# Sums of squares on quarters of the array, and a new order of the first loads, in a one-core decoder layer

## The reference

```python
mod = silu(c) @ w_ada + b_ada                      # shift1, scale1, gate1, shift2, scale2, gate2
h = x * (1 + scale1) + shift1
q, k, v, u_a, v_a = split(h @ w_in)                # each 1024 wide
attn = moba_attention(q, k_all, v_all, rel_bias)   # 8 heads; sample rows also see 256 cached rows
gm = gelu(u_a) * chunk_spatial_gate(layer_norm(gelu(v_a)))
mixed = concat(rms_norm(gm) * norm_a_g, rms_norm(attn) * norm_b_g)
x = layer_norm(ALPHA * x + gate1 * (mixed @ w_out))
h = x * (1 + scale2) + shift2
up = h @ w_up;  ff = silu(conv_a(up)) * conv_b(up) # causal convolution, width 3, d_ff 5504
y = layer_norm(ALPHA * x + gate2 * (ff @ w_down))
```

## Time and profile before

| | us |
|---|---|
| median of 3 executions | 1412.66 (1411.91 to 1414.5) |
| the profiled execution | 1412.51 |
| its span, first to last instruction | 1410.1 |
| TensorE busy | 1373.4 (97%) |
| VectorE busy | 841.1 (60%) |
| ScalarE busy | 569.1 (40%) |
| GpSimd busy | 103.7 (7%) |

### The profile page before, as it was taken

One profiled execution on the slowest core, in us unless ns is written; L12 is line 12 of the kernel. 1 busy time (PEld: TensorE's weight loads), 2 busy tenths in 40 slices (PEclk: granted clock), 3 DMA queues, 4 the chain that ended last, 5 costly groups with the idle time before them and its releaser, 6 DMA issues.

```text
span 1410.1 us, 29096 instructions
## 1 busy us (share of the span) xinstructions
PE 1373.4 (97%) x11354; PEld 1300.6 (92%) x11354; DVE 841.1 (60%) x1400; ACT 569.1 (40%) x842; POOL 103.7 (7%) x250
## 2 busy tenths in 40 slices
PE   5999999999999999999999999999999999999996
PEld 4989898899788888899999999999999999999995
DVE  2475556567866458565666454675665544766655
ACT  3532222253543236643444333444444333444443
POOL 1000000003221000110001000010010000101000
PEclk9999999999999999999999999999999999999997
DMA  9989988885789989775544545545545454454541
GB/s 374 380 334 383 344 337 310 331 284 170 258 280 336 340 308 345 266 284 212 187 156 158 173 162 164 163 149 178 164 146 182 158 168 162 147 181 166 173 136 67
DMA packets 89762, 324.92 MB, mean 230 GB/s; under 512 B 10637, under 2 KB 10637, under 8 KB 89296
## 3 DMA queue, kind: packets, MB, share of 16 engines
q1 hardware_dynamic: 82368, 297.05, 59.3%
q0 software_dynamic: 6880, 24.10, 4.9%
q10 hardware_dynamic: 432, 2.62, 0.5%
HBM read 318.05 MB, written 5.67 MB: 230 GB/s over the span
## 4 chain that ended last, share of the span: by engine, by line
PE 93%; DVE 2%; DMA 2%; ACT 1%; issue 1%; SPq 1%; DVEq 0%; ACTq 0%
PE ps L446 28%; PE ps L447 28%; PE ps L448 27%; PE ps L462 5%; DMA ada<-w_ada 1%; DMA raw<-w_in 1%; PE ps L753 1%; PE ps L624 0%; SPq L895 0%; ACT wH L973 0%; DVE wL L1356 0%; PE ps L554 0%; PE ps L651 0%; PE ps L672 0%; PE ps L475 0%
## 5 line engine op out<-in xcount | busy, mean ns | idle before, releaser
L1356 DVE TENSOR_TENSOR wL<-raw,wH 128x1024 fp32r<-128x1024 f32 x372 | 449.0, 1217 | 358.3 <-ACT wH L973 356.4
L973 ACT ACTIVATE wH<-raw 128x1024 fp32r<-128x1024 f32 x372 | 389.5, 1053 | 587.4 <-PE ps L448 568.3
L446 PE MATMUL ps<-hL,wH 128*128 128x288 f32 x2016 | 602.6, 299 | 5.0 <-DVE hL L1394 4.4
L447 PE MATMUL ps<-hH,wL 128*128 128x288 f32 x2016 | 600.4, 298 | 0.0
L448 PE MATMUL ps<-hH,wH 128*128 128x288 f32 x2016 | 598.6, 297 | 0.0
L446 PEld LDWEIGHTS ps<-hL,wH 128*128 128x128 f32 x2016 | 381.6, 189 | 19.2 <-issue 9.8
L447 PEld LDWEIGHTS ps<-hH,wL 128*128 128x128 f32 x2016 | 379.4, 188 | 0.5 <-issue 0.5
L448 PEld LDWEIGHTS ps<-hH,wH 128*128 128x128 f32 x2016 | 379.1, 188 | 0.0
L446 PE MATMUL ps<-ffL,wH 128*128 128x288 f32 x688 | 204.5, 297 | 0.0
L447 PE MATMUL ps<-ffH,wL 128*128 128x288 f32 x688 | 203.0, 295 | 0.0
L448 PE MATMUL ps<-ffH,wH 128*128 128x288 f32 x688 | 202.3, 294 | 0.0
(11 more groups left out here) (237 smaller groups left out, 1005.3 us busy)
## 6 DMA issues: line engine op xcount, KB each, us to landing
raw<-w_up SPq DMA_DIRECT2D x168, 512.0 KB, 3.5
ada<-w_ada SPq DMA_DIRECT2D x112, 512.0 KB, 6.2
raw<-w_down SPq DMA_DIRECT2D x83, 512.0 KB, 3.5
raw<-w_in SPq DMA_DIRECT2D x80, 512.0 KB, 7.5
adaX<-w_ada SPq DMA_DIRECT2D x40, 512.0 KB, 5.4
adaY<-w_ada SPq DMA_DIRECT2D x40, 512.0 KB, 7.3
raw<-w_out SPq DMA_DIRECT2D x32, 512.0 KB, 5.3
KV<-keys POOLq DMA_DIRECT2D x16, 512.0 KB, 5.6
```

Source lines behind the costliest of these rows:

```text
L446: nc.tensor.matmul(out, wH[:, w:w + P], rhs_lo(kk), start=start, stop=False)
L447: nc.tensor.matmul(out, wL[:, w:w + P], rhs_hi(kk), start=False, stop=False)
L973: nc.scalar.activation(wH[:, o:o + cols], raw[:, o:o + cols], ACT.Copy).then_inc(hi_done, 1)
L1356: vec_tt(wL[:, o:o + cols], raw[:, o:o + cols], wH[:, o:o + cols].bitcast(F32), ALU.subtract).then_inc(split_done, 1)
```

## The change

At the start:

- SyncE issues `w_in` slab 0 between the fourth and the fifth conditioning slab. The first rows of x come in two loads: tiles 0 and 1 on SyncE's queue after the eighth conditioning slab, tiles 2 and 3 on ScalarE's queue after the high part of slab 1.
- ScalarE and VectorE split slab 0 before the modulation. `modulate` does the samples first and then each k-tile's prompt part as one tensor_scalar (multiply and add), and for k-tile 0 and 1 the high part, the low part and TensorE's wait are made tile by tile (`h32_first`, `hH_first`, `h_first`). ScalarE's high part of slab 1 comes after these.
- The first two bursts come after slab 3 and slab 6, not 2 and 5; the turn of unit 1 moves from slab 6 to 7.

At the end of the input projection:

- "sum a" becomes eight matmuls with 32 columns of ones, four at a time on the four column quarters of the array (`quarter_sums`), a copy of the 128 rows of partial sums by ScalarE, and one full matmul over them (`joined_sums`); each sum is then 32 times too large, which the root's scale undoes. "sum ad" likewise. The samples' squares move from step 79 to 78; the quarters of "sum ad" come after slab 78, its joined sum after slab 79.
- The joined sum of "sum a" comes after slab 78. VectorE inverts the root and does `norm_prompt(0, 0)` at step 78. `norm_prompt(0, 1)` moves behind the split of slab S_OUT + 3, and `m_ready` now counts it, so mix tiles 4 to 7 wait for it and tiles 0 to 3 don't.
- `turn_v` uses banks 2, 3, 4 and then 5, 4, 3; the second three come after `past_scores(0)`. `scores(0)` waits for two groups, not four. `new_scores` comes after `out_slab(0)`, and its VectorE part (`new_logits`) after the mix tiles 4 to 7.
- GpSimd's second product comes right behind its first, ahead of the store of k and of the load of the second cached sequence.

```diff
-BURSTS = [2, 5, 8, 11, 14, 16] + [...]
+BURSTS = [3, 6, 8, 11, 14, 16] + [...]
...
@@ tensor
+            def quarter_sums(job, bank, ready, lo, hi):
+                pe.wait_ge(sq_ready, ready)
+                b = take(pe, job, bank)
+                for j in range(2):
+                    for c in range(4):
+                        mm = nc.tensor.matmul(b[32 * c:32 * c + 32, lo:hi], ones[:, 0:32], tile(proj, 32 + 4 * j + c, lo, hi), start=(j == 0), stop=(j == 1))
+                fill(mm, job)
+            def joined_sums(job, parts_job, bank, parts, lo, hi):
+                released(pe, parts_job)
+                b = take(pe, job, bank)
+                fill(nc.tensor.matmul(b[:, lo:hi], ones[:, :], parts, start=True, stop=True), job)
...
-                if g == 0:
+                if i == 0:
+                    arriving = lambda kk: pe.wait_ge(h_ready if kk else h_first, 1)
+                elif g == 0:
...
                 if i == 77:
-                    sum_squares("sum a", 5, 1, [tile(proj, k, 0, SEQ) for k in range(32, 40)], 0, SEQ)
-            turn_v(0, 0, 0)
-            turn_v(1, 0, 6)
-            turn_v(2, 0, 7)
-            sum_squares("sum ad", 5, 2, [tile(proj, k, SEQ, ROWS) for k in range(32, 40)], SEQ, ROWS)
+                    quarter_sums("quarters a", 5, 1, 0, SEQ)
+                if i == 78:
+                    joined_sums("sum a", "quarters a", 6, RRa[:, :], 0, SEQ)
+                    quarter_sums("quarters ad", 5, 2, SEQ, ROWS)
+            joined_sums("sum ad", "quarters ad", 7, RRd[:, :], SEQ, ROWS)
+            turn_v(0, 0, 2)
+            turn_v(1, 0, 3)
+            turn_v(2, 0, 4)
...
@@ sync
             for a in range(HALF):
+                if a == HALF // 2:
+                    load(0, io["w_in"], 0, 0)
                 load_ada(a, a)
-            for s in range(RING):
+            sp.dma_start(xT[:, 0:2 * ROWS], io["xT"][:, 0:2 * ROWS]).then_inc(x_in, 16)
+            for s in range(1, RING):
                 load(s, io["w_in"], s, s)
...
@@ scalar
-                if i == 79:
+                if i == 78:
+                    b = filled(act, "quarters a")
+                    release(nc.scalar.activation(RRa[:, :], b[:, 0:SEQ], ACT.Copy), "quarters a")
                     square_a(SEQ, ROWS, 3).then_inc(sq_ready, 1)
-                    root(0, "sum a", 0, SEQ)
+                    root(0, "sum a", 0, SEQ, 1.0 / 32)
+                    b = filled(act, "quarters ad")
+                    release(nc.scalar.activation(RRd[:, :], b[:, SEQ:ROWS], ACT.Copy), "quarters ad")
...
-                act.wait_ge(m_ready, 1 if k < 8 else k // 4)
+                act.wait_ge(m_ready, 1 + k // 4)
...
-            act.dma_start(xT[:, 0:4 * ROWS], io["xT"][:, 0:4 * ROWS]).then_inc(x_in, 16)
             act.wait_ge(c_in, 16)
             nc.scalar.activation(cT[:, :], cT[:, :], ACT.Silu).then_inc(c_silu, 1)
+            hi(0, 0, 0)
             unit_copy(0)
-            hi(0, 0, 0)
+            act.wait_ge(h32_first, 1)
+            nc.scalar.activation(tile(hH, 0), tile(H32, 0), ACT.Copy).then_inc(hH_first, 1)
+            act.wait_ge(h32_ready, 1)
+            nc.scalar.activation(tile(hH, 1), tile(H32, 1), ACT.Copy).then_inc(hH_ready, 1)
             hi(1, 0, 1)
-            h_hi(0)
+            act.dma_start(xT[:, 2 * ROWS:4 * ROWS], io["xT"][:, 2 * ROWS:4 * ROWS]).then_inc(x_in, 16)
             hi(2, 0, 2)
...
@@ vector
+                steps.link(vec_tt(dd, by_seq(tiles(xT, k, 2, SEQ, ROWS), 2), scale, ALU.mult))
+                vec_tt(dd, dd, shift, ALU.add)
+                for t in range(2):
+                    ins = vec_ts(tile(H32, slot + t, 0, SEQ), tile(xT, k + t, 0, SEQ), modT[:, a:a + 1], modT[:, b:b + 1], ALU.mult, ALU.add)
+                    if p == 0 and t == 0:
+                        ins.then_inc(h32_first, 1)
+                ins.then_inc(h32_ready, 1)
...
                 if i == 78:
                     invert_root(0, "sum a", 0)
-                if i == 79:
                     norm_prompt(0, 0)
-                    norm_prompt(0, 1)
...
+            lo(0, 0)
             mod_finish(("turn", 0), (0, 16), n=2)
             dve.wait_ge(x_in, 16)
             modulate(0)
-            lo(0, 0)
-            h_lo(0)
...
             lo(S_OUT + AHEAD, AHEAD)
-            ...
+            norm_prompt(0, 1).then_inc(m_ready, 1)
             own_queries(1)
...
                     for k in range(4, 8):
                         mix_lo_at(k)
+                    new_logits()
...
@@ gpsimd
             nc.gpsimd.tensor_tensor(VAs[:, :], VAs[:, :], SG[:, :], ALU.mult).then_inc(vas_done, 1)
+            pool.wait_ge(vas_done, 1)
+            nc.gpsimd.tensor_tensor(VAs[:, :], VAs[:, :], SH[:, :], ALU.add).then_inc(vas_done, 1)
             in_done(pool, 8)
```

67 lines of the change are left out of this document (38 added, 29 removed).

## The result

The changed kernel takes 1407.57 us (median of 16 runs, 1404.6 to 1411.51), the kernel before in the same runs 1411.48 us (1409.88 to 1414.5). The ratio is 0.997 with a 95% interval of 0.9963 to 0.9977: 3.9 us or 0.3% faster (0.9970 x 1411.48 is 1407.2). The forecast was 1407.7 us, "faster" by more than 0.2%, with a range of 1405.6 to 1410.8. The profiled execution of the changed kernel took 1408.39 us with a span of 1406.7, against 1412.51 and 1410.1.

The account below looks back on a forecast made before the run. TensorE, busy 1373.4 of 1410.1 us, was taken as the bound. 4.9 us from the earlier out slab plus 1.6 from its clock, less 0.3, 0.9 and 0.3, net 5.0: 1412.66 - 5.0 = 1407.7 us, range 1405.6 to 1410.8.

Parts of the forecast that it names:

- The start: Input projection's beginning: slab 0 starts near 20.0, 2.2 us earlier, but TensorE still goes on at 31.6; no gain.
- Value 0: Gain taken for slab 0's earlier beginning: 0 us, since slab 4 lands at 30.2 again; upper bound 0.6 us gained.
- The clock at the start: Rival, chance 0.25: TensorE's wait before 31.6 grows to 1.8 to 2.8 us, the clock falls, costing 1.6 us; time 1409.3.
- The sums: End of input projection: "sum a" costs 1.4 us, TensorE reaches slabs 78 and 79 2.0 us earlier, slab 79 ends near 350.7.
- the delay of 1.0 us: VectorE's split at 342.63 and all after it run 1.0 us late beside GpSimd's moved second product; bounds 0 and 1.1.
- The way to the first out slab: VectorE's operations from slab 81's split to the mix tiles, added up: `out_slab(0)` starts at 357.5 instead of 362.4.
- Behind it: After the first out slab: full clock, TensorE waits 0.9 us for probabilities, whose turn starts at 362.0, 5.2 us won.
- The 0.3 us: Up to 0.3 us lost at `attend(0)`, with ScalarE late through its table load and four mix tiles.

Follow-up runs that it names:

- start_alone: The kernel before with only the changes at the start; ratio 1.0004 to the kernel before.
- banks_first: The changed kernel with ScalarE emptying slab 1's banks before taking slab 4's high part; ratio 0.9952 to the kernel before.
- longer_wait: The changed kernel with an extra GpSimd load of the cached rows (0.70 MB) ahead of slab 4's load; ratio 0.9995 to the kernel before.
- pool_late: The changed kernel with GpSimd's second product back behind the store of k and the second cache load; ratio 0.9999 to the kernel before.
- new_logits_first: The changed kernel with VectorE's `new_logits` ahead of mix tiles 4 to 7; ratio 0.9964 to the kernel before.
- logits_keys: The changed kernel with `new_logits` ahead of mix tiles 4 to 7 and the second cached sequence loaded before k's store; ratio 1.0002 to the kernel before.

## Why the prediction was right, and where it was off

**The start: right in value, off in one term.** Value 0 was taken because slab 4's landing sets when TensorE goes on; start_alone has a ratio of 1.0004, and slab 4's high part stands at 30.19, 30.28 and 30.34 in three kernels. That its landing hangs on the bytes ahead of it was shown from both sides, by 460 KB less (29.37) and 688 KB more (32.59). The term off is slab 0's start, 20.65 instead of 20.0. The steps from the modulation on took what was added up: VectorE has the modulation's inputs at 18.7, the first k-tile at 19.5 and its low part at 20.5. What came late was the conditioning phase ahead of it: the last 16 matmuls of it took 1.08 us in after, at a granted clock of 0.50, and 0.65 in the trace of before at 1.00, and its last turn starts at 17.95 instead of 17.55. The same turn starts at 18.75 in start_alone. This cost nothing, as it stands ahead of a stop. The prediction said in passing that ScalarE "sits in its own order" and then summed as though the load were the limit; for the sum both are one, for the next change they are not (banks_first).

**The clock at the start: right in the trace.** The stop is 1.82 us, inside the 1.8 to 2.8 of the forecast, and the clock stays at 1.00 behind it. In longer_wait it fell at this place, after 3.25 us of idle time. What the forecast did not have is that it was already at 0.50 from 16 to 24 us and that slab 0 ran at that pace.

**The sums: right.** "sum a" was to cost 1.4 us; its quarters are 1.07 and the joined sum 0.60, 1.67 together. VectorE's split takes 2.22 us, the delay of 1.0 us that was taken. Between slab 78 and 79 TensorE was to wait 0.4; the joined sum fills that time, and the wait is under 0.1. Slab 79 was to end near 350.7 and ended at 351.0, with 0.3 us of that brought along from the start.

The Trainium skill ("SBUF — State Buffer", Who interferes with whom) has the exclusive lock between GpSimd and VectorE's operations with two inputs in SBUF. The runs agree, for the tensor_tensor too: 2.22 us with the product beside it, 1.22 in pool_late without. They show the other direction as well: in pool_late it is GpSimd's product that is held up, 5.34 instead of 2.37 us, over several operations of VectorE in a row.

**The way to the first out slab: right.** The forecast was 357.5, the trace has 357.73. The steps on VectorE, against the forecast: reciprocal done at 349.9 (349.7), `norm_prompt` 351.1 (350.8), additions 352.6 (352.3), split 353.7 (353.5), mix tiles 357.7 (357.4). Each is 0.2 to 0.3 late, the 0.26 us that the changed kernel is behind at 320 us. The full clock is there in this trace, and the probabilities' turn starts at 362.17 (362.0).

**Behind it: one term mis-sized.** The 0.3 us "at `attend(0)`, where ScalarE comes through its table load and four mix tiles late" are 1.17 us, and the engine is another one. `new_scores` moved behind the first out slab and holds its bank until `new_logits`, and the change put that behind mix tiles 4 to 7 on VectorE, 1.80 us. The prediction had costed the moved matmuls (0.34 us), but neither the moved vector part nor the bank that it frees. It was also wrong about the keys: their second pair is issued 1.4 us earlier than before (356.38 against 357.82), not about 3, and new_logits_first shows a wait of 0.99 us for them hidden behind the bank's. With 0.9 us more there and 0.26 from the start, the 5.0 us of the forecast become 3.8, which is what the traces show at `past_scores(1)`, and 3.9 is what the medians show. The forecast of 1407.7 was counted from a median of 1412.66 over 3 runs; over 16 runs that of the kernel before is 1411.48, and this 1.2 us made good the error of 1.1. That the time agrees to 0.1 us is therefore luck: the saving was 3.9 us and not 5.0.

**A cause the prediction had too small.** It priced GpSimd's second product at its new place by what it costs there, 1.0 us, and had its old place as the reason for one slow mix tile of 1.44 us. pool_late shows that the rest of the change needs the move: with VectorE full, the product at the old place takes 5.34 us, VectorE's own wait for it (`vas_done`) holds the probabilities up, and the gain is gone. The prediction did not name that wait. The sum was right only because the move is in the change.

**Open.** That the quarters' 2.0 us and the rest of the end (4.05 in all) add up was not tested part by part; pool_late shows that they do not simply add, since one part missing cancels the others. How often the clock falls is not known, neither after a stop of three microseconds (the profiled execution of longer_wait lost 4.0 us to it, all its executions together some 1.2 us on average, 3.5 less 2.25) nor at the first attention, where waits of the same length had it at 1.00 in the changed kernel and at 0.50 in longer_wait. What sets when the slow pace at the start ends, 24.0 to 26.8 us, is open too.

## What to carry to other kernels

An engine that runs in order should empty the bank that TensorE waits for before it waits for a load, if what that load brings is needed only later: a start made earlier is worth nothing as long as such an order stands behind it, here nothing without the turn, and some 1.5 us of the 2.05 between two traces with it. When an operation is moved behind another engine's work, follow the buffer that it holds until then as well as its own duration. And a GpSimd product belongs where VectorE has no row of two-input work and no engine waits for the product soon after: the same one cost 1.0 us on VectorE in one place and the whole gain of the change in another. A single trace is one execution: before a difference between two traces is credited to an edit, compare the pace of the matmuls and the places where the edit changes nothing.

## What the runs showed of the hardware

- A GpSimd tensor_tensor of 32 x 1024 took 2.37 to 2.40 us in before and after. Beside it, VectorE's 128 x 1024 tensor_tensor took 2.22 us in after, and 1.22 in pool_late without it. In pool_late the product took 5.34 us: it started into a row of VectorE's operations, none of which was stretched, and ended 2.23 us after their end.
- TensorE's clock was at 0.50 after 3.08, 3.22 and 3.25 us of idle time in pool_late, logits_keys and longer_wait, and at 1.00 after 1.82 us in the changed kernel and 0.88 in start_alone. Waits of 0.44, 0.73 and 1.17 us left it at 1.00 in the changed kernel, and behind 0.44, 0.73 and 1.16 it was at 0.50 in longer_wait.
- At the start matmuls of 288 columns ran 0.24 us apart up to 24.0 to 26.8 us in thirteen traces and 0.13 apart from there. The last 16 conditioning matmuls took 1.08 us in after and 0.65 in before.
- 460 KB less on GpSimd's queue brought a load of SyncE's queue 0.97 us earlier, and 688 KB more 2.25 us later, with the DMA engines full (share about 1.0).
- Eight sums with 32 columns of ones on column quarters took 1.07 us for 256 columns plus 0.60 for the joined sum, where full matmuls took 3.61 in the same place, and 0.33 us for 32 columns where those took 1.86.
